# Dense products that read their moving operand from the last column to the first

## The reference

```
mod  = silu(c) @ w_ada + b_ada                     # 2048 x 12288
proj = (rms_norm(x) * (1+scale) + shift) @ w_in    # 2048 x 5456
x   += gate * rms_norm([diff_attention, indexed_sparse_attention] @ w_o)
ff   = (silu(h @ w_gate) * (h @ w_up)) @ w_down    # 5632 wide
x   += gate_f * rms_norm(ff)
# second block: 16 meta tokens are put ahead, so 272 tokens
proj = rmsnorm(h) @ w_in_2                         # 2048 x 3904
h   += [neighbourhood_attention, mla_attention] @ w_out_2
h   += conv_glu(rmsnorm(h), w_gate_2, w_up_2, conv_w_2, conv_b_2, w_down_2)
```

## Time and profile before

| | us |
|---|---|
| median of 3 runs | 2589.59 |
| profiled execution | 2586.09 |
| its span, first to last instruction | 2584.3 |
| TensorE matmul busy (share of the span) | 2479.3 (96%) |
| TensorE weight load busy | 2348.3 (91%) |
| VectorE busy | 1439.8 (56%) |
| ScalarE busy | 1032.9 (40%) |
| GpSimd busy | 290.8 (11%) |
| mean granted TensorE clock | 0.979 of full speed |

### The profile page before, as it was taken

How to read it: one execution, slowest core, us unless ns; L and a number is a source line. 1 busy time by engine, 2 the same in 40 slices (tenths; PEclk the granted TensorE clock), 3 DMA queues, 4 the chain that set the end, 5 groups by cost and what they waited for, 6 DMA issues and landing times.

```text
span 2584.3 us, 47889 instructions
## 1 busy us (share of the span) xinstructions
PE 2479.3 (96%) x20022; PEld 2348.3 (91%) x20022; DVE 1439.8 (56%) x1926; ACT 1032.9 (40%) x1332; POOL 290.8 (11%) x372
## 2 busy tenths in 40 slices
PE   6999988989999999999989998998999999999999
PEld 4999857979999999999979997878999999999999
DVE  3687657966764444443455554755655555554443
ACT  3533244344333434333334445443444444443333
POOL 5000122410100000011113002113000000000000
PEclk8999989989999999999989999999999999999999
DMA  9887865977785555555544442314455555555553
GB/s 345 290 289 267 292 211 173 334 274 244 249 291 192 186 187 184 184 180 181 189 135 150 148 153 66 115 66 131 148 179 188 181 182 178 179 182 181 190 181 130
DMA packets 263862, 504.24 MB, mean 195 GB/s; under 512 B 17152, under 2 KB 26283, under 8 KB 263467
## 3 DMA queue, kind: packets, MB, share of 16 engines
q1 hardware_dynamic: 257899, 494.97, 57.0%
q10 hardware_dynamic: 5840, 7.52, 0.9%
HBM read 498.04 MB, written 2.10 MB: 194 GB/s over the span
## 4 chain that ended last, share of the span: by engine, by line
PE 80%; DVE 8%; ACT 4%; issue 4%; DMA 2%; SPq 1%; POOL 1%; DVEq 0%; ACTq 0%; POOLq 0%
PE bank L2110 24%; PE bank L2112 24%; PE bank L2111 24%; ACT w_hi L935 3%; DVE w_lo L1458 3%; PE bank L2145 2%; DMA raw<-in_w_in 1%; DVE tmp L1592 1%; DVE ada_acc L1486 1%; DMA staged<-in_w_ada 1%; SPq L646 1%; PE bank L2254 1%; SPq L739 1%; PE bank L2455 0%; ACT x_hi L1046 0%
## 5 line engine op out<-in xcount | busy, mean ns | idle before, releaser
L1458 DVE TENSOR_TENSOR w_lo<-raw,w_hi 128x2048 fp32r<-128x2048 f32 (+3 forms) x386 | 863.5, 2237 | 942.2 <-ACT w_hi L935 941.7
L2110 PE MATMUL bank<-x_hi,w_hi 128*128 128x256 f32 (+2 forms) x4608 | 1317.5, 286 | 35.6 <-DVE w_lo L1458 19.1
L2112 PE MATMUL bank<-x_hi,w_lo 128*128 128x256 f32 (+2 forms) x4608 | 1307.6, 284 | 0.0
L2111 PE MATMUL bank<-x_lo,w_hi 128*128 128x256 f32 (+2 forms) x4608 | 1301.2, 282 | 0.0
L935 ACT ACTIVATE w_hi<-raw 128x2048 fp32r<-128x2048 f32 (+3 forms) x386 | 718.7, 1862 | 1032.8 <-PE bank L2112 905.8
L2110 PEld LDWEIGHTS bank<-x_hi,w_hi 128*128 128x128 f32 x4608 | 873.0, 189 | 71.9 <-issue 40.7
L2111 PEld LDWEIGHTS bank<-x_lo,w_hi 128*128 128x128 f32 x4608 | 873.1, 189 | 1.2 <-issue 1.2
L2112 PEld LDWEIGHTS bank<-x_hi,w_lo 128*128 128x128 f32 x4608 | 872.2, 189 | 0.0
L2112 PE MATMUL bank<-hid_hi,w_lo 128*128 128x256 f32 x1408 | 397.0, 282 | 0.0
L2110 PE MATMUL bank<-hid_hi,w_hi 128*128 128x256 f32 x1408 | 394.1, 280 | 2.8 <-DVE w_lo L1458 1.5
L2111 PE MATMUL bank<-hid_lo,w_hi 128*128 128x256 f32 x1408 | 394.3, 280 | 0.0
(11 more groups left out here) (332 smaller groups left out, 1462.6 us busy)
## 6 DMA issues: line engine op xcount, KB each, us to landing
raw<-in_w_gate SPq DMA_DIRECT2D x88, 1024.0 KB, 5.2
raw<-in_w_up SPq DMA_DIRECT2D x88, 1024.0 KB, 5.2
raw<-in_w_ada SPq DMA_DIRECT2D x72, 1024.0 KB, 6.7
raw<-in_w_in SPq DMA_DIRECT2D x68, 1024.0 KB, 5.7
raw<-in_w_down SPq DMA_DIRECT2D x64, 1024.0 KB, 5.0
raw<-in_w_down SPq DMA_DIRECT2D x32, 768.0 KB, 4.3
beside<-in_w_ada SPq DMA_DIRECT2D x16, 1024.0 KB, 7.5
raw<-in_w_o SPq DMA_DIRECT2D x16, 1024.0 KB, 6.7
```

The source lines that it names most:

```text
L1458: dve.tensor_tensor(w_lo[ps][:, 0:width], raw[slot][:, 0:width], w_hi[ps][:, 0:width], ALU.subtract).then_inc(raw_free[slot], 1)
L2110: pe.matmul(out, wh[:, k, c], hi(k0 + k), start=a0, stop=False)
L2111: pe.matmul(out, wh[:, k, c], lo(k0 + k), start=False, stop=False)
L2112: ins = pe.matmul(out, wl_[:, k, c], hi(k0 + k), start=False, stop=z)
```

## The change

In `dense`, the moving operand and the output are both viewed with a step of -1 along the tokens. Column n-1 of the activations is read first and written to column n-1 of the bank first; column 0 comes last. Every product goes to the same element of the bank as before, so the sums are the same. The weights, the order of the instructions, their number and their semaphores are not touched. All three matmuls of each (m, k) are changed, and no matmul outside `dense`.

```diff
-                        out = (banks(m) if banks else bank[base + m])[0:r, 0:n]
+                        out = (banks(m) if banks else bank[base + m])[0:r, 0:n][:, ::-1]
...
-                            pe.matmul(out, wh[:, k, c], hi(k0 + k), start=a0, stop=False)
-                            pe.matmul(out, wh[:, k, c], lo(k0 + k), start=False, stop=False)
-                            ins = pe.matmul(out, wl_[:, k, c], hi(k0 + k), start=False, stop=z)
+                            pe.matmul(out, wh[:, k, c], hi(k0 + k)[:, ::-1], start=a0, stop=False)
+                            pe.matmul(out, wh[:, k, c], lo(k0 + k)[:, ::-1], start=False, stop=False)
+                            ins = pe.matmul(out, wl_[:, k, c], hi(k0 + k)[:, ::-1], start=False, stop=z)
```

## The result

The changed kernel ran at a median of 2592.13 us (20 runs, 2586.08 to 2595.32), the kernel before at 2587.02 us (20 runs, 2581.43 to 2594.16). The ratio is 1.0018, with a 95% interval from 1.0011 to 1.0026. So it is slower, clear of noise, by 4.7 us (the two medians lie 5.1 us apart). That is within the 0.2% band of the forecast, and 2.1 us from the forecast time.

The account below looks back on a forecast made before the run. TensorE's dense matmul pitch was taken to bound the kernel. All terms summed to 0 us against the profiled 2586.1 us; with the median of the runs 3.5 us above that, the forecast was 2590 us, range 2535 to 2700.

Parts of the forecast that it names:

- 0.2% band: Whole kernel: a difference within 5.2 us, about what a measurement can tell from no change; mean pitch within 0.29 ns.
- What bounds the kernel: TensorE, busy 96% of the span: 18048 dense matmuls, 1 ns of pitch being 18.0 us, 0.70%.
- Readers: Readers of the bank wait for the tile's last matmul, not for a column: 0 us.
- accumulation: Adding to the bank: distance between two writes of one element stays n columns: 0 us.
- other engines: Outside TensorE: no new bound at lower pitch, just longer waits at higher pitch; sum 0 us.
- The rate of reading and writing backwards: Columns in each dense matmul: taken as the old rate, 0 us, between ends of -118 and +1740 us.
- Rival C: Dense matmuls: writing or reading backwards runs at half rate, +1740 us, 4330 us in all; chance 0.16.
- The 10 to 12 ns above the columns: Matmul pitch beyond its columns, perhaps from the next weight read: taken as 0 us, ends -118 and +144 us.
- rival A: Dense matmuls at full clock: order worsens interlock of weight and moving read; +1.5 ns gives 2617 us; chance 0.25.
- no change: Whole kernel: no measurable change, the direction costing nothing or the reversals folded away; 2590 us, chance 0.38.
- B: Dense matmuls: order improves the interlock; -1.5 ns gives 2563 us, the end of 112 ns 2472; chance 0.21.
- D: Whole change: the two reversals cancel and are folded away before the chip, 2590 us; chance 0.05.

Follow-up runs that it names:

- shift32: Kernel before with x_hi, x_lo, hid_hi, hid_lo and all behind them 32 bytes further on, weight buffers staying: 1.0064 of before.
- shift_all32: Kernel before with everything, weight buffers and moving operands alike, 32 bytes further on: 1.0003 of before.
- back_shift32: Changed kernel with x, hid and all behind them 32 bytes further on, weight buffers staying: 1.0030 of before.
- shift64: Kernel before with x, hid and all behind them 64 bytes further on, weight buffers staying: 1.0031 of before.
- shift128: Kernel before with x, hid and all behind them 128 bytes further on, weight buffers staying: 1.0006 of before.
- write_back: Kernel before with only the bank written from last column to first, moving operand read in rising order: 0.9996 of before.
- pairs: Kernel before with moving operand and bank walked in rising pairs, second column of each pair first: 1.0005 of before.

## Why the prediction was right, step by step

*What bounds the kernel.* Right, and what made the rest readable: 18048 dense matmuls at the pitch, 18.0 us for each ns. Over all fourteen kernels the mean pitch ranges from 118.46 to 119.70 ns and the time follows it: shift32 has +1.13 ns, which makes 20 us by that factor, and measured +16.6 (the spans differ by 16.9). A line through the fourteen profiled executions rises by 15 us for each ns, somewhat less than 18.0.

*Readers, accumulation, other engines: 0 us.* Right. Writing the bank backwards alone measured 0.9996.

*The rate of reading and writing backwards: 0 us*, taken between -118 and +1740 us. Right: the pitch is 117.8 ns at granted clock 1.00. Rival C, with 0.16, was the least grounded chance; its page says that a non-contiguous PSUM pattern slows matmuls significantly (SBUF — State Buffer, Door 1: The DMA port swizzle, of the Trainium skill). By these runs (0.9996 and 1.0005) a step of -1 and swapped pairs don't count as such.

*The 10 to 12 ns above the columns: 0 us, ends -118 and +144.* The value was right to 0.34 ns, 6 us of span, and the reason given for the width was the mechanism: two states 1.1 ns apart at the same addresses, weight read against moving read. It was called a guess there; shift32 against shift_all32 bears it out. What I did not see is that before ran in the better state for part of its `x` products, so that a reordering had something to lose: the spread was read as having no sign. A look at which products were in which state would have given a hint: about half of them stood at the lowest mean that is seen in any kernel, 116.7 ns, so there was more to lose than to win. The ends were far too wide: all kernels measured lie between -0.05% and +0.64%.

*The cases.* By the profile it is rival A that happened (+0.34 ns is beyond the +0.29 ns from which A was said to decide), by the runs it is 0.18% and inside the band of no change. Both are the same 5 us; the border between the two cases ran through the result. A's price of +27 us for 1.5 ns was not reached by any kernel. B's 112 ns was reached by single pitches only. D, that the change does nothing, is out: the patterns are new.

*What was luck.* The 2590 us rest on a median of three runs, 2589.59 us; over 20 runs the kernel before has 2587.02. The base was 2.6 us too high, and this brought the forecast nearer to the slower result: what was forecast is no change, and the change is 5 us. That a shift with a size and a sign fixed by where the buffers lie came out this small was luck too; with the same backward order at other places, back_shift32 is 0.30% above the kernel before.

*Against the rule on two ports.* The Trainium skill (TensorE: Matmul & The Clock Gate, Step-by-step: what each phase is for) says that loading the next weights takes no read bandwidth from the running matmul. Here 32 bytes between the two reads raise the mean pitch by 1.1 ns (by 1.6 ns for `x` of 256 columns) and 32 bytes on both leave it as it was, to within 0.1 ns. So at the high clock level the two reads are not independent. The forecast kept its own ends against that page, rightly.

## What to carry to other kernels

A tuned matmul stream can have a cost of some ns per matmul that no wait shows; look at the starts, not at busy time, and see whether the pitch repeats with k. If it does, the places of moving operand and weights modulo 256 bytes are a knob worth up to 0.6% here, and any change that moves a buffer by 32 or 64 bytes may turn it unasked: compare pitches before explaining a difference of a few tenths of a per cent by the change itself. Writing the bank backwards cost nothing that could be measured. Reading backwards did no more than move the matmuls to another of these patterns: slower at one place, not slower at another.

## What the runs showed of the hardware

The mean pitches of undisturbed 256-column products are not arbitrary. Nearly all fall on few values, 116.7, 117.8, 118.3, 118.9, 120.0 and, in `hid` of shift64, 121.1 ns (119.3, in two `hid` products of shift128, is another). For the three matmuls of a k that is 350.0, 353.3, 355.0, 356.7, 360.0 and 363.3 ns, at 2.4 GHz 840, 848, 852, 856, 864 and 872 cycles: all multiples of four (119.3 ns is not), where 768 are columns. Four columns of float32r are 16 bytes. That is the line that the Trainium skill gives for SBUF (SBUF — State Buffer, Door 1: The DMA port swizzle). The swapped pairs keep each column within its four, and leave the mean pitches alone too. All this would fit a stream that loses whole lines to the other one, but that is a guess: no run shows the lines, and why there is a floor of 840 stays open. At the 1.2 GHz level the changed kernel has no such cost; its timeline, start us:

```profile
285.73 0.41 PE L2110 MATMUL bank<-x_hi,w_hi 128*128 128x256 f32 x1
...
287.65 0.41 PE L2110 MATMUL bank<-x_hi,w_hi 128*128 128x256 f32 x1
```

Nine matmuls in 1.92 us, 213 ns each, as in the earlier trace rows. What decides which state a product falls into after a wait was not settled; kernels with the same places (before, write_back, pairs, shift_all32) take it differently in the same product.
